# Order of the z loads and of the convolution's chunks, contiguous constants for TensorE, dummy products in the routing, and the last expert pair summed in PSUM

## The reference

```python
h = rms_norm(x, g_mix_pre)
z = jnp.matmul(h, w_in)                 # 1024 -> 3200 columns
rq, rk, rv, rg, aq, ak, av, gu, gv = jnp.split(z, cuts, axis=-1)
# rotation of rq, rk, aq, ak; retention; dilated attention; spatial gating
x = x + rms_norm(jnp.matmul(y, w_out), g_mix_post)
gate, up = jnp.split(jnp.matmul(rms_norm(x, g_ffn_pre), w_gate_up), [FFN_HIDDEN], axis=-1)
x = x + rms_norm(jnp.matmul(jax.nn.silu(gate) * up, w_down), g_ffn_post)
```

```python
mod = jnp.split(silu(c) @ w_ada + b_ada, 6)          # shifts and scales, for c and c_ctx
z, xbc, dt_raw, u, gates = jnp.split(modulate(x, *mod) @ w_in, IN_SPLITS, axis=-1)
xbc = silu(conv_centred(xbc, conv_w, conv_b))        # 5 taps per channel
xs, bm, cm = jnp.split(xbc, ...)                     # 2048, 512, 512 channels
dt = softplus(dt_raw + dt_bias); a = -dt * exp(a_log)
# state-space scan in both directions, starting from the context's states; a pooling branch
x = layer_norm(ALPHA * x + mod_2 * merged @ w_out)
# 32 experts, the 2 best of one group per token: segment_sum(swiglu(x[tokens of e]) * weight)
return layer_norm(ALPHA * x + mod_5 * experts(x))
```

## Time and profile before

| | us |
|---|---|
| three runs | 1688.23, 1692.65, 1696.2 |
| median | 1692.65 |
| the profiled execution's own time | 1690.42 |
| its span | 1688.6 |
| TensorE busy | 1608.7 (95%) |
| VectorE busy | 779.1 (46%) |
| ScalarE busy | 605.9 (36%) |
| GpSimd busy | 476.1 (28%) |

### The profile page before, as it was taken

The page is one execution under the profiler, slowest core; times in us unless marked ns, Lnnn a source line. Parts: engine busy times, 40 slices in busy tenths (PEclk is TensorE's granted clock), DMA queues, the critical chain, the costliest instruction groups (busy, mean ns, idle before and its releaser), DMA issues.

```text
span 1688.6 us, 24295 instructions
## 1 busy us (share of the span) xinstructions
PE 1608.7 (95%) x9875; PEld 1227.5 (73%) x9875; DVE 779.1 (46%) x1288; ACT 605.9 (36%) x1088; POOL 476.1 (28%) x305
## 2 busy tenths in 40 slices
PE   6999999999999999999999999999899999999994
PEld 5888999868889998888777889899544444444442
DVE  4645333246463232378765566446533333332224
ACT  3544444334453333455445556334211111111110
POOL 4633444433234444400024565344300000000000
PEclk9999999999999999999999999999799999999998
DMA  7643997526439886433222333847799999999993
GB/s 256 200 150 114 261 263 229 175 93 228 137 101 273 250 250 223 138 101 100 75 75 76 100 101 113 282 134 235 320 426 421 424 421 422 423 422 423 422 422 144
DMA packets 244261, 397.87 MB, mean 236 GB/s; under 512 B 6725, under 2 KB 195585, under 8 KB 223280
## 3 DMA queue, kind: packets, MB, share of 16 engines
q1 hardware_dynamic: 237360, 365.45, 62.4%
q10 hardware_dynamic: 3760, 20.85, 3.1%
q0 software_dynamic: 3024, 9.95, 1.7%
HBM read 395.17 MB, written 1.05 MB: 235 GB/s over the span
## 4 chain that ended last, share of the span: by engine, by line
PE 78%; DMA 10%; DVE 7%; POOL 2%; issue 2%; ACT 1%; ACTq 0%; DVEq 0%; POOLq 0%; SPq 0%
PE ps L143 77%; DMA arena<-in_w_expert_up 4%; DMA ring<-in_w_expert_gate 4%; DVE arena L153 2%; PE ps L145 2%; DVE split_r L149 1%; DVE arena L149 1%; DMA ring<-in_w_out 1%; POOL split_r L149 1%; ACT split_r L147 1%; POOL small L169 1%; DMA ring<-in_w_in 1%; DMA X<-in_x 1%; DVE arena_r L149 0%; ACT arena L147 0%
## 5 line engine op out<-in xcount | busy, mean ns | idle before, releaser
L143 PE MATMUL ps<-arena_r,split_r 128*128 128x256 f32 (+1 forms) x2984 | 460.4, 288 | 2.3 <-POOL split_r L149 2.3
L149 POOL TENSOR_TENSOR split_r<-ring,split_r 128x1024 fp32r<-128x1024 f32 (+1 forms) x142 | 334.1, 2355 | 330.0 <-ACT split_r L147 321.0
L143 PEld LDWEIGHTS ps<-arena_r,split_r 128*128 128x128 f32 x2984 | 394.0, 189 | 19.3 <-issue 14.1
L147 ACT ACTIVATE split_r<-ring 128x1024 fp32r<-128x1024 f32 (+1 forms) x293 | 296.2, 1019 | 306.0 <-PE ps L143 219.7
L149 DVE TENSOR_TENSOR split_r<-ring,split_r 128x1024 fp32r<-128x1024 f32 (+1 forms) x151 | 211.4, 1402 | 317.0 <-ACT split_r L147 309.3
L143 PE MATMUL ps<-split_r,arena_r 128*128 128x512 f32 (+1 forms) x1520 | 343.7, 379 | 3.1 <-issue 1.7
L143 PE MATMUL ps<-arena 128*64 128x512 f32 (+8 forms) x1472 | 310.2, 458 | 12.8 <-DMA arena<-in_w_expert_up 4.2
L143 PEld LDWEIGHTS ps<-split_r,arena_r 128*128 128x128 f32 x1520 | 276.0, 189 | 51.9 <-issue 8.0
L143 PEld LDWEIGHTS ps<-arena 128*64 128x64 f32 (+2 forms) x1472 | 138.2, 151 | 136.1 <-issue 120.0
L143 PE MATMUL ps<-hhh_r,split_r 128*128 128x256 f32 (+1 forms) x976 | 222.4, 316 | 0.0
L143 PE MATMUL ps<-ring,arena 128*64 128x512 f32 (+2 forms) x768 | 213.3, 579 | 8.1 <-DVE arena L149 2.4
(11 more groups left out here) (158 smaller groups left out, 1259.1 us busy)
## 6 DMA issues: line engine op xcount, KB each, us to landing
ring<-in_w_gate_up SPq DMA_DIRECT2D x88, 512.0 KB, 7.4
arena<-in_w_expert_up SPq DMA_DIRECT2D x15, 2048.0 KB, 29.3
arena<-in_w_expert_gate SPq DMA_DIRECT2D x15, 2048.0 KB, 29.1
ring<-in_w_expert_down SPq DMA_DIRECT2D x15, 2048.0 KB, 31.7
ring<-in_w_in SPq DMA_DIRECT2D x57, 512.0 KB, 5.1
ring<-in_w_expert_gate SPq DMA_DIRECT2D x13, 2048.0 KB, 27.0
arena<-in_w_ada SPq DMA_DIRECT2D x24, 1024.0 KB, 7.0
ring<-in_w_down SPq DMA_DIRECT2D x22, 1024.0 KB, 5.0
```

The source lines that it names most:

```text
L143: made = e.matmul(*a, **k)
L147: made = e.activation(*a, **k)
L149: made = e.tensor_tensor(*a, **k)
```

## The change

- The units of z are loaded in the order 1, 0, 2 to 7; TensorE's order of products is the same.
- The convolution's chunks go x 0-3, B 0-3, x 4-7, C 0-1, x 8-15, C 2-3. `dt_sums` stands behind chunk 10 and what follows it one chunk later; the states' weights and sums stand where their chunks are done; no chunk is left to transpose at the end.
- VectorE writes w_ada's units 6 to 9 in the order in which TensorE reads them, so that the weights are contiguous.
- `turn_over` issues products of two constants whose result nobody reads: 4, 14 and 5 of them in the routing.
- Pair 0's transposes of the one-hots, its slots' weights and the counts go behind the first part of its `gate_up`.
- For the last pair TensorE puts `YA` itself into the four banks (a product with the identity), adds the pair's result to it by halves, and VectorE takes the statistics from PSUM; ScalarE copies the sums to `YA`.

```diff
-CONV_UNITS = [0, 4, 5, 1, 2, 3]
+CHUNKS = [0, 1, 2, 3, 16, 17, 18, 19, 4, 5, 6, 7, 20, 21, 8, 9, 10, 11, 12, 13, 14, 15, 22, 23]
+WEIGHTED, SUMMED, KEPT = {12: 0, 15: 1, 20: 2}, {14: 0, 17: 1, 22: 2}, {15: 0, 18: 1, 23: 2}
...
-        for u, (c0, n) in enumerate(Z_UNITS):
+        for u in (1, 0, *range(2, len(Z_UNITS))):
+            c0, n = Z_UNITS[u]
...
# ada_sums
-                        part = by_four(AD[u % 2])[:, :, c] if u // 2 in (3, 4) else AD[u % 2][:, tok(c)]
-                        made = t.matmul(bk[:, 2 * c:2 * c + 2], part, C("selc"), True, True)
+                        made = t.matmul(bk[:, 2 * c:2 * c + 2], AD[u % 2][:, tok(c)], C("selc"), True, True)
# products_kept
+                if u // 2 in (3, 4):
+                    then(v.copy(in_fours(AD[u % 2]), by_four(B("am", u))), ("am", u, "kept"))
...
# convolution, TensorE
-                    if m == 9:
+                    if m == 10:
                         dt_sums()
-                    if m in (15, 19, 23):
-                        state_sum((m - 15) // 4)
-                to_tokens(22)
+                    if m in SUMMED:
+                        state_sum(SUMMED[m])
                 projected(0)
-                to_tokens(23)
                 projected(1)
...
+            def turn_over(key, n):
+                bk = take(("over", key))
+                for _ in range(n):
+                    t.matmul(bk[:, 0:P], ident, ones, True, True)
...
# routing: behind the transposes of the first 128 tokens, behind both logits, behind the rank
+                    if i == 0:
+                        turn_over(0, 4)
+                turn_over(1, 14)
+                turn_over(2, 5)
...
# gate_up
                         if part == 0 and p:
                             combine(p - 1)
+                        elif part == 0:
+                            slots(0)
+                            if r == 0:
+                                counts()
...
+                def sums(h, x):
+                    bk = take(("ya", r, 15, h, x), ("ya", r, 15, h, x, "kept"), ("full", r, h, x), hold=True)
+                    t.wait_ge(*at("ya", r, 14, h, x, "kept"))
+                    t.matmul(bk, ident, YA[:, x, half(h)], True, False)
+                def combine_last(h):
...
+                    for x in range(2):
+                        bk = B("ya", r, 15, h, x)
+                        t.matmul(bk, ONET[:, 1, tok(x)], OEH[:, half(h)], False, False)
+                        t.matmul(bk, ONET[:, 1, tok(x)], OEL[:, half(h)], False, True).then_inc(*sig(s_done, ("ya", r, 15, h, x)))
+                        drop(("ya", r, 15, h, x))
...
# the last pair: sums(0, 0) and sums(0, 1) around turn_products, then
-                combine(15)
+                combine_last(0)
+                for x in range(2):
+                    sums(1, x)
+                combine_last(1)
...
# VectorE's end
-                combined(15)
+                for h in range(2):
+                    for x in range(2):
+                        v.wait_ge(*at("ya", r, 15, h, x))
+                        then(v.bn_stats(BN[:, x, h, :], B("ya", r, 15, h, x)), ("ya", r, 15, h, x, "kept"))
# ScalarE's end
+                for h in range(2):
+                    for x in range(2):
+                        s.wait_ge(*at("ya", r, 15, h, x, "kept"))
+                        s.activation(YA[:, x, half(h)], B("ya", r, 15, h, x), ACT.Copy).then_inc(*sig(s_done, ("full", r, h, x)))
```

More of the change, by code:

```diff
@@ L262, in weights @@
     columns("dt", win2, 5120, 1)
-    for u in CONV_UNITS:
-        columns(f"conv{u}", win2, 2048 + u * 512, 4)
+    for m in range(0, 24, 2):
+        columns(f"conv{m}", win2, 2048 + CHUNKS[m] * P, 2)
     begin("merged")
@@ L395, in by_vector @@
                     return True
[L396 removed]
+                if first["z", l, 1][1] <= n < first["down", l][1] + 22:
                     return n % 2 == 0
@@ L1214, in gather, with slots @@
                     made.then_inc(*sig(s_done, ("hg", r, p, q)))
-                    if q == 0:
-                        return
+                def slots(p):
+                    i = p % 2
                     bk = take(("pw", r, p), ("pw", r, p, "kept"))
@@ L1281, in experts @@
                         gather(p + 1, 0)
+                    else:
+                        sums(0, 0)
                     turn_products(p)
@@ L1284, in experts @@
                         gather(p + 1, 1)
+                        slots(p + 1)
+                    else:
+                        sums(0, 1)
                     down(p)
-                combine(15)
+                combine_last(0)
+                for x in range(2):
+                    sums(1, x)
+                combine_last(1)
             t.wait_ge(*at("ident"))
@@ L1539, in activate @@
                     if c < 20:
-                        if m >= 3 and 4 * CONV_UNITS[(m - 3) // 4] + (m - 3) % 4 < 20:
-                            s.wait_ge(*at("tk", m - 3))
+                        for k in [k for k in range(m - 3, -1, -3) if CHUNKS[k] < 20][:1]:
+                            s.wait_ge(*at("tk", k))
                         s.activation(TCS[m % 3], CA[:, i, 0, :], ACT.Silu, bias=gcol(40 + c, 1))
@@ L2556, in experts, with part_low @@
                     then(v.copy(AT, fold(B("av", r, p), 4)), ("av", r, p, "kept"))
+                    def part_low(h):
+                        v.wait_ge(*at("oeh", r, p, h))
+                        then(v.tensor_tensor(OEL[:, half(h)], OE[:, 0, half(h)], OEH[:, half(h)], ALU.subtract), ("oel", r, p, h))
                     for h in range(2):
@@ L2562, in experts @@
                         then(v.stt(OE[:, 0, half(h)], B("oe", r, p, h), WSL[:, i:i + 1], MG[:, 0, half(h)], ALU.mult, ALU.mult), ("oe", r, p, h, "kept"))
-                    for h in range(2):
-                        v.wait_ge(*at("oeh", r, p, h))
-                        then(v.tensor_tensor(OEL[:, half(h)], OE[:, 0, half(h)], OEH[:, half(h)], ALU.subtract), ("oel", r, p, h))
-                combined(15)
+                        if p == 15:
+                            part_low(h)
+                    if p < 15:
+                        for h in range(2):
+                            part_low(h)
+                for h in range(2):
+                    for x in range(2):
+                        v.wait_ge(*at("ya", r, 15, h, x))
+                        then(v.bn_stats(BN[:, x, h, :], B("ya", r, 15, h, x)), ("ya", r, 15, h, x, "kept"))
+                if r == 0:
+                    for x in range(2):
+                        variance(2, x, s_done)
             then(v.memset(negh[:, :], -0.5), ("neg",))
@@ L2880, in sync @@
                     y.wait_ge(*at("am", u))
-                load_to(first["z", 1, 0][0] if l == 0 else n1)
+                load_to(first["z", 1, 1][0] if l == 0 else n1)
             load_to(first["end",][0])
```

76 lines of the change are left out of this document (35 added, 41 removed).

## The result

The changed kernel takes 1672.86 us by median of four runs (1671.03 to 1678.76), beside 1693.2 for the kernel before; the ratio estimated from the runs is 0.9895 (0.9868 to 0.9921; the two medians alone give 0.988). In a second comparison of six runs it is 1674.17, ratio 0.9898 (0.9879 to 0.9916). The forecast was 1671.7, range 1664 to 1681. The profiled execution of the changed kernel took 1673.52 (span 1671.7), 16.9 under the profiled one of before; by its own terms the forecast wanted 20.9 there. So the time was hit and the working was not: one of its terms came out less than half, one is partly paid back at the far end, and another was bigger than forecast. The stages show which.

A forecast was written before the change was run, and what follows sets the result against it. TensorE was taken as the bound, its own work holding 78% of the chain. Terms 1.1 + 3.7 + 6.1 + 3.8 + 3.7 + 2.5 = 20.9 off the profiled 1690.42 gave 1669.5; with 2.2 for the median, 1671.7, range 1664 to 1681.

The forecast's parts named there:

- z's loads: Loading z's unit 1 first closes TensorE's holes before unit 2: gain 1.1 in layer 0, 3.7 in layer 1.
- The collision rival: GpSimd's split and VectorE's rotation collide in layer 1: 1.1 to 1.6 not won, 1672.8 to 1673.3; chance 0.12.
- The convolution: New chunk order removes TensorE's 3.87 wait before the sums of dt and most clock loss: gain 6.1, 3.9 to 7.3.
- the 1.2 that I kept back as lost: Part of the convolution's 3.4 clock loss behind the wait, assumed to remain because busy narrow products also showed clock 0.74.
- w_ada's order: Layer 1's w_ada sums read contiguous weights instead of strided: gain 3.8, 3.0 to 3.8; VectorE's permuted copies cost 0.
- Routing and slots: Unread products raise the routing's clock, and pair 0's slots and counts move later: gain 3.7, from -2.5 to 4.6.
- Last pair: At the kernel's end VectorE's four adds go and the norm starts earlier: gain 2.5, 1.0 to 3.2.
- The expert stream doesn't absorb: Against the rival that bytes fix the expert stream's end, so only the tail's 2.5 shows: 1690.2; chance 0.05.
- VectorE never bound the changed convolution: Against the slower rival: VectorE bounds the convolution's full chunks, 30 lost against 20.9, 1702; chance 0.03.
- The clock doesn't follow: Rival: holes don't set the clock, so layer 1, convolution and routing lose their clock gains; gain 14.5, 1678.1; chance 0.24.

The follow-up runs named there:

- only_z: The kernel before with the new order of z's loads alone; 1682.82 us, ratio 0.9944.
- conv_old: The changed kernel with the convolution's chunks back in the old order; 1675.94 us, ratio 0.9916.
- carry_late: The changed kernel with the summed dt's transposes, their copies and subtractions moved from behind chunk 11 to behind chunk 16; 1670.42 us, ratio 0.9867.
- after_again: The changed kernel itself, unaltered, run once more beside two other kernels on one chip; 1674.17 us.
- slots_first: The changed kernel with slots and counts ahead of pair 0's first half product again; 1672.67 us, ratio 0.9886.
- all_fill: last_fill with unread products in three more holes: 20 instead of 14 before the rank, 9 before the scan, 8 before layer 1's raw half; 1662.83 us.
- last_fill: carry_late with expert load 2 issued behind branch b and 12 unread products in the last pair's hole; 1668.59 us, ratio 0.9848.

## Why the prediction was right, and where it wasn't

**z's loads: right in mechanism, too small.** Forecast 1.1 + 3.7 = 4.8, measured 1.70 + 3.25 + 1.28 = 6.2 (only_z and every kernel with the edit agree). In both layers I left 1.0 for the six transposes; without a hole ahead of them they cost the next group 0.4, as 37.61 to 38.01 shows. The collision rival's price was off as well: the rotation's four operations take 1.96 in both layers now, 0.7 more than in layer 0 before and 0.9 less than in layer 1 before, and nobody waits for them, since the load comes early enough. The time goes with how long GpSimd's split runs beside it: not at all in layer 0 before (1.29), for 0.8 now (1.96), for its whole 1.87 in layer 1 before (2.89). The Trainium skill's rule (SBUF — State Buffer, "SBUF: two separate sides") that VectorE with two SBUF inputs and GpSimd shut each other out fits these three; no run here separates it.

**The convolution: the step that failed.** I wrote that the 3.87 "goes whole" and with it most of the clock. The hole went, as said, and the clock with it: from 784.10 to 793.10 it is 1.00, so even the 1.2 that I kept back as lost was not lost. What I left out is ScalarE. I checked only that VectorE had room, and counted the moved transposes and copies as "the same in number". They are, and ScalarE's three table loads in 8 us are the same too. What changed is who waits for its queue. Before, this work stood among chunks of C, which are not transposed, and the next activated chunk that TensorE needed was due at 816.43, 11 us behind the last table load. Now chunk 11 is one of x: TensorE transposes it two chunks later, and these two are the light ones (2.8 each). TensorE ran dry for 3.17, and had clock 0.68 over the 5.35 behind it, 1.7 lost. Forecast 6.1, measured 2.8 in the stage; conv_old shows the size, carry_late the cause: with the copies among full chunks the stage saves 7.7, the 4.9 of wait and clock more, and more than the forecast's upper bound of 7.3. At the scan's start the changed kernel has clock 0.79 over 8 us (before: 1.00), behind a wait of 2.21 that was there before too; 0.21 x 8 = 1.7 of the longer "to hm" is this window:

```profile
891.40:899.40 8.00, 8.00 (x54) 6.51 (x54) 6.70 (x14) 6.11 (x16) 4.71 (x2) 0.79 0.25 69
```

**w_ada's order: right.** 3.8 forecast, 3.84 measured ("-conv": 343.07 with z's edit alone, 339.23 with both in after_again). VectorE's four permuted copies grew by (6.5 - 4.8) / 4 = 0.4 each and are hidden.

**Routing and slots: right up to the issue, then partly given back.** Forecast 3.7; SyncE's issue came 4.3 to 4.6 nearer to hm in the two profiles of the changed kernel. From the issue to the down products both take 1.9 to 2.2 longer than before: 0.8 to 1.0 in the stream, which the forecast took for untouched, and 1.1 to 1.2 in the last part, at 9.90 and 9.98 instead of 8.78 behind its hole. Net 2.7 and 2.1. slots_first, with the slots in the old place, is without this loss, so the slots' move seems to give back the 1.0 it wins; it is one profile, and part of the loss is the last part's clock.

**Last pair: right.** 2.5 forecast, 8.44 to 5.45 is 3.0, within 0.03 in eleven profiles. It is about the four adds (2.7 in the earlier trace rows).

**Sum.** 6.2 + 2.8 + 3.8 + 2.7 + 3.0 = 18.5, less 2.4 of "to hm", plus 1.7 in the raw half (neither belongs to an edit), less 0.7 of a later start: 17.1, beside the 16.98 between the norms' starts (1678.77 and 1661.79). The medians lie 20.3 and 17.8 apart in the two comparisons; the kernel before alone runs from 1685 to 1700. The forecast's 20.9 had the convolution 3.3 too high, the routing 1.0 too high, and z and the tail 1.9 too low. That the median still met it is luck: the medians lie 3.4 further apart than the two profiled executions, and the median of before in the first comparison, 1693.2, lies 1.2 to 3.6 above those of the three others. A time that fits doesn't show that the terms do.

**The rivals.** The expert stream doesn't absorb: the issue moved by 15.9 and the last down products by 14.0. VectorE never bound the changed convolution: ScalarE did, at one place. "The clock doesn't follow" was half right: where a hole went it followed each time (layer 1's unit 2 and the sums of dt in all profiles, the last pair in both), and in four other places (raw half, scan's start, first gather, last part) it differed between alike kernels.

## What to carry over

When a step moves, list every engine that works in it, and ask at the new place who waits next for that engine's queue and how much work lies over it until then; table loads on ScalarE count as work. The same ScalarE work was free where no chunk had to be transposed behind it (before), free among full 5.9 us chunks (carry_late), and cost 3 us where a result was due two light chunks of 2.8 us later. And read several profiles of alike code before believing a stage: here four stages change by 1.6 to 7 us with nothing changed in them, while the edits' own stages repeat within 0.1 to 0.7.

## What the runs showed of the hardware

The clock falls behind holes of 2 to 4 us, but not behind each of them each time: layer 1's second raw half stands behind a wait of 2.33 to 2.36 in twelve profiles, and took 4.97 to its next group in five of them and 6.55 to 6.67 in seven, with nothing different ahead of it in the instructions. With the hole filled it was at 4.97 in the one profile there is (all_fill), which the other profiles' chance could give as well. The Trainium skill's rule of no TensorE-idle gaps (TensorE: Matmul & The Clock Gate, "HAM oscillation — how this bites in real kernels"), which I discounted in the forecast, is borne out at the last pair: its 32 records took 8.65 to 9.98 in the eleven profiles with the hole and 7.09 in the two where it is filled (last_fill, all_fill).

A 512 KB load of the ring that takes 6.0 to 6.9 when issued 1.5 to 2.0 ahead of a 2 MB expert load on another queue took 11.0 to 12.9 when issued 0.4 to 1.1 ahead of it (three profiles of nine); the chain of waits names it, the averages on the page of the profile don't. Why the lead matters no run here shows.
